# Dilated attention with the tokens stored by residue: fewer score blocks, and the two heads of a pair on the two halves of the array

## The reference

```python
ATTN_GROUPS = ((128, 1), (512, 4), (2048, 16))
...
    s = jnp.einsum('brhnqd,brhnkd->brhnqk', qb, kk) * (dh ** -0.5) + bias
    s = jnp.where(valid, s, -jnp.inf)
    mx = jnp.max(s, axis=-1, keepdims=True)
    p = jnp.exp(s - mx)
    l = jnp.sum(p, axis=-1)
    o = jnp.einsum('brhnqk,brhnkd->brhnqd', p, vv) / l[..., None]
    lse = mx[..., 0] + jnp.log(l)
...
    wts = jax.nn.softmax(jnp.stack(lses, axis=0), axis=0)
    y_b = jnp.sum(wts[..., None] * jnp.stack(outs, axis=0), axis=0)
```

## Time and profile before

| | |
|---|---|
| median of 3 runs | 2230.58 us |
| the profiled execution, its span | 2225.15 us, 2223.2 us |
| busy share of the span: PE, DVE, ACT, POOL | 96%, 48%, 30%, 13% |
| mean granted TensorE clock | 0.983 of 2.4 GHz |
| attention stage (the four pairs) | 404 to 736 us from the start |

### The profile page before, as it was taken

How to read it: one execution, slowest core, us unless ns; L and a number is a source line. 1 busy time by engine, 2 the same in 40 slices (tenths; PEclk the granted TensorE clock), 3 DMA queues, 4 the chain that set the end, 5 groups by cost and what they waited for, 6 DMA issues and landing times.

```text
span 2223.2 us, 24553 instructions
## 1 busy us (share of the span) xinstructions
PE 2144.5 (96%) x9948; PEld 1713.2 (77%) x9948; DVE 1077.8 (48%) x1707; ACT 656.9 (30%) x1069; POOL 295.0 (13%) x214
## 2 busy tenths in 40 slices
PE   6999999999999999999998899999999999999997
PEld 5777788777777888888877567777777778888886
DVE  6566543444445644343454655235555644434344
ACT  4333322222223432222233222023343334222222
POOL 3122210111111111010020001120010112001012
PEclk9999999999999999999998999899999999999998
DMA  4222233322221333333321222231111132333331
GB/s 146 70 76 76 81 112 98 79 69 69 72 78 38 95 91 99 95 96 104 93 79 60 67 67 67 76 105 47 48 48 39 48 104 69 102 95 95 99 91 67
DMA packets 53312, 178.33 MB, mean 80 GB/s; under 512 B 5975, under 2 KB 7255, under 8 KB 53200
## 3 DMA queue, kind: packets, MB, share of 16 engines
q1 hardware_dynamic: 52480, 175.61, 26.0%
q10 hardware_dynamic: 720, 1.16, 0.1%
HBM read 174.46 MB, written 2.28 MB: 79 GB/s over the span
## 4 chain that ended last, share of the span: by engine, by line
PE 90%; DVE 6%; ACT 2%; issue 1%; POOL 0%; DMA 0%; SPq 0%; DVEq 0%; POOLq 0%
PE PS L881 25%; PE PS L883 24%; PE PS L882 24%; PE PS L1016 2%; PE PS L1039 2%; PE PS L1143 2%; PE PS L1170 2%; PE PS L1025 1%; PE PS L1118 1%; PE PS L994 1%; PE PS L981 1%; DVE WL L1454 1%; PE PS L1096 1%; PE PS L946 1%; PE PS L1078 1%
## 5 line engine op out<-in xcount | busy, mean ns | idle before, releaser
L881 PE MATMUL PS<-HH,WH 128*128 128x512 f32 x1368 | 561.1, 410 | 14.6 <-DVE WL L1454 11.9
L883 PE MATMUL PS<-HH,WL 128*128 128x512 f32 x1368 | 538.2, 393 | 0.0
L882 PE MATMUL PS<-HL,WH 128*128 128x512 f32 x1368 | 536.8, 392 | 0.0
L881 PE MATMUL PS<-AH,WH 128*128 128x512 f32 x1096 | 445.1, 406 | 10.4 <-DVE WL L1454 8.5
L1454 DVE TENSOR_TENSOR WL<-RAW,WH 128x1024 fp32r<-128x1024 f32 (+2 forms) x257 | 324.9, 1264 | 256.9 <-ACT WH L1214 256.4
L1214 ACT ACTIVATE WH<-RAW 128x1024 fp32r<-128x1024 f32 (+2 forms) x320 | 325.4, 1017 | 365.0 <-PE PS L883 316.6
L883 PE MATMUL PS<-AH,WL 128*128 128x512 f32 x1096 | 431.9, 394 | 0.0
L882 PE MATMUL PS<-AL,WH 128*128 128x512 f32 x1096 | 431.5, 394 | 0.0
L881 PEld LDWEIGHTS PS<-HH,WH 128*128 128x128 f32 x1368 | 259.2, 189 | 79.5 <-issue 14.4
L883 PEld LDWEIGHTS PS<-HH,WL 128*128 128x128 f32 x1368 | 258.9, 189 | 56.4
L882 PEld LDWEIGHTS PS<-HL,WH 128*128 128x128 f32 x1368 | 259.9, 190 | 50.0 <-issue 1.0
(11 more groups left out here) (224 smaller groups left out, 1794.9 us busy)
## 6 DMA issues: line engine op xcount, KB each, us to landing
RAW<-wst SPq DMA_DIRECT2D x296, 512.0 KB, 3.5
RAW<-wst SPq DMA_DIRECT2D x16, 384.0 KB, 3.0
AR<-scr SPq DMA_DIRECT2D x16, 256.0 KB, 4.5
RAW<-wst SPq DMA_DIRECT2D x16, 256.0 KB, 2.5
XT<-xT SPq DMA_DIRECT2D x3, 512.0 KB, 8.1
AR<-scr SPq DMA_DIRECT2D x8, 128.0 KB, 5.3
out<-XT SPq DMA_DIRECT2D x4, 256.0 KB, 2.0
out<-XT ACTq DMA_DIRECT2D x4, 256.0 KB, 2.1
```

The lines of the kernel that those rows point to most:

```text
L881: T.matmul(out, wh, XH[:, k, :], start=k == 0, stop=False)
L882: T.matmul(out, wh, XL[:, k, :], start=False, stop=False)
L883: m = T.matmul(out, wl, XH[:, k, :], start=False, stop=k == nk - 1)
```

## The change

Groups 1 and 2 have dilations 4 and 16, so a query meets only keys of its own residue modulo 4. Their q, k and v are now stored by residue: DVE writes the evicted sums of these units through a view that puts the four residues one after the other (`by_residue`), and a block of 128 then holds one residue. A query block needs two blocks of group 0 (one for the first), one of group 1 and one of group 2: 15 blocks a head. An item is now a pair and a block b, with both heads.

Each matmul of a step is issued for head 0 and then head 1. For the scores the heads lie on the two halves of the partitions and write two banks; for the products with the values the value block (64 columns) is stationary, the turned probabilities (128 columns) move, and the heads write the two halves of the partitions of one bank. The result stands turned already, so `turn_yb` goes.

A query block of group 0 holds other tokens than one of groups 1 and 2, so there are two softmaxes, with their own maxima and sums, and `merge` joins them in three steps once a pair: `choose_strips` (DVE) and `unfold` (one matmul, then eight dependent DVE instructions with one exponential on ACT) bring the second softmax's statistics into token order and give each its share; `shares` spreads them with 16 matmuls of a column by the identity, and `split_yb` multiplies, adds and splits. For a pair this stands within the first block of the next one, for the last pair at its end.

`Fill` has 10 places for nine units (18 for the eight of the last pair), not 26 weighted ones, and before the scores of the next pair's first block the units are drained. A bias vector has 384 values and is made in one piece. The table of constants grows by 136 columns.

```diff
-        for p in range(2):
-            e.turn_bank("vector", g, p)
-            e.bias_vector(g, p)
+        e.turn_bank("vector", g)
+        e.bias_vector(g)
...
+def merge(e, hp, step):
+
+    if step == 0:
+        e.choose_strips(hp)
+    elif step == 1:
+        e.hold(4, "unfolded", hp)
+        e.unfold(hp)
+    elif step == 2:
+        for x in (0, 1):
+            e.turn_bank("share", hp, x)
+        e.shares(hp)
+        e.split_yb(hp)
+
+
+def ask(e, hp, b):
+    for i in (0, 1):
+        e.hold(SB[i], "qk", hp, b, i)
+    e.attention_scores(hp, b)
...
 def attention_pair(e, hp, units):
-    items = [(hp, i, n) for i in (0, 1) for n in ORD_N]
-    fill = Fill(e, units, 26)
-
-    def ask(it):
-        for g in range(3):
-            e.hold(SB[g], "qk", it, g)
-        e.attention_scores(it)
-
-    ask(items[0])
-    e.attention_softmax(items[0])
-    for m, it in enumerate(items):
-        w = WORK[it[2]]
-        then = items[m + 1] if m < 7 else None
-        fill(w)
-        if then:
-            ask(then)
-        fill(w)
-        blocks = 2 * (it[2] + 1) + min(2, it[2] + 1)
-        for b in range(0, blocks, 4):
-            if b == 8:
-                fill(w)
-            e.turn_bank("turn", it, b)
-            e.attention_turn(it, b, min(4, blocks - b))
-        if then:
-            e.attention_softmax(then)
-        fill(w)
-        e.hold(OB, "pv", it)
-        e.attention_out(it, blocks)
+    fill = Fill(e, units, 10 if hp < 3 else 18)
+    for b in range(4):
+        if hp and b == 0:
+            merge(e, hp - 1, 0)
+        fill()
+        if b < 3:
+            ask(e, hp, b + 1)
+        elif hp < 3:
+            fill.drain()
+            ask(e, hp + 1, 0)
+        if hp and b == 0:
+            merge(e, hp - 1, 1)
+        fill()
+        for i in (0, 1):
+            e.turn_bank("turn", hp, b, i)
+            e.attention_turn(hp, b, i)
+        if b < 3:
+            e.attention_softmax(hp, b + 1)
+        elif hp < 3:
+            e.attention_softmax(hp + 1, 0)
+        if hp and b == 0:
+            merge(e, hp - 1, 2)
+        fill()
+        e.hold(OB, "pv", hp, b)
+        e.attention_out(hp, b)
+        if hp == 3 and b == 3:
+            for step in range(3):
+                merge(e, 3, step)
+                fill(2)
     fill.drain(hp == 3)
-    e.turn_bank("yb", hp)
-    e.turn_yb(hp)
...
+    ask(e, 0, 0)
+    e.attention_softmax(0, 0)
...
+            def bias_vector(s, g):
+                b = s.bank["vector", g]
+                s.free("vector", g)
...
+                t = T.matmul(PS[0:24, b, 0:384], tab[0:33, :], oh[0:33, g * 384:(g + 1) * 384], start=True, stop=True)
...
-            def attention_scores(s, it):
-                hp, i, n = it
-                sl, W, k0, p = SLOT[hp % 2], 128 * (n + 1), max(0, n - 1), slice(64 * i, 64 * i + 64)
+            def attention_scores(s, hp, b):
+                sl = SLOT[hp % 2]
                 for g in range(3):
                     pe.wait_ge(*at("free", "sum", unit_of("ka", 4 * g + hp)))
-                for x, (g, ka, w) in enumerate(((1, 0, W), (2, 0, W), (0, k0 * 128, W - k0 * 128))):
+                s.free("qk", hp, b, 0)
+                s.free("qk", hp, b, 1)
+                for g, k, n, a in ((0, max(0, b - 1), min(2, b + 1), score_column(b)), (1, b, 1, 256), (2, b, 1, 384)):
                     o = 3 * g * 512
-                    s.free("qk", it, x)
-                    t = T.matmul(PS[:, SB[x], 0:w], sl[p, o + n * 128:o + n * 128 + 128],
-                                 sl[p, o + 512 + ka:o + 512 + ka + w], start=True, stop=True)
-                    t.then_inc(*pe_done["attn"].next("scored", it, x))
-
-            def attention_turn(s, it, m, c):
-                b, Sx = s.bank["turn", it, m], SS[ORD_N.index(it[2]) % 2]
-                s.free("turn", it, m)
-                pe.wait_ge(*at("p", it))
-                for q in range(c):
-                    t = T.transpose(PS[:, b, q * 128:(q + 1) * 128], Sx[:, (m + q) * 128:(m + q + 1) * 128], ident())
...
-            def attention_out(s, it, blocks):
-                hp, i, n = it
-                s.free("pv", it)
...
+                t.then_inc(*pe_done["attn"].next("p_turned", hp, b, i))
+
+            def attention_out(s, hp, b):
+                s.free("pv", hp, b)
                 for g in range(3):
                     pe.wait_ge(*at("free", "tokens", unit_of("va", 4 * g + hp)))
-                keys = [(1, j) for j in range(n + 1)] + [(2, j) for j in range(n + 1)] + \
-                       [(0, j) for j in range(max(0, n - 1), n + 1)]
-                for m, (g, j) in enumerate(keys):
-                    if m % 4 == 0:
-                        pe.wait_ge(*at("free", "turn", it, m))
-                    o = (3 * g + 2) * 512 + j * 128 + 64 * i
-                    t = T.matmul(PS[:, OB, 0:64], PT[:, m * 128:(m + 1) * 128], SLOT[hp % 2][:, o:o + 64], start=m == 0,
...
+                pe.wait_ge(*at("free", "turn", hp, b, 0))
+                pe.wait_ge(*at("free", "turn", hp, b, 1))
+                blocks = [(0, 0, b - 1, b > 0, False), (0, 128, b, b == 0, True), (1, 256, b, True, False),
+                          (2, 384, b, False, True)]
+                for g, c, j, first, last in blocks[b == 0:]:
+                    o, x = (3 * g + 2) * 512 + j * 128, min(g, 1) * 128
+                    for i in (0, 1):
+                        t = T.matmul(PS[64 * i:64 * i + 64, OB, x:x + 128], SLOT[hp % 2][:, o + 64 * i:o + 64 * i + 64],
+                                     PT[:, 512 * i + c:512 * i + c + 128], start=first, stop=last)
+                t.then_inc(*pe_done["attn"].next("pv", hp, b))
...
+            def unfold(s, hp):
+                s.free("unfolded", hp)
+                pe.wait_ge(*at("strips", hp))
+                t = T.matmul(PS[:, 4, 0:64], con("unfold"), strips, start=True, stop=True)
...
+            def shares(s, hp):
+                pe.wait_ge(*at("share", hp))
+                for x in (0, 1):
+                    b = s.bank["share", hp, x]
+                    s.free("share", hp, x)
+                    for n in range(4):
+                        for i in (0, 1):
+                            c = 8 * x + 2 * n + i
+                            t = T.matmul(PS[64 * i:64 * i + 64, b, n * 128:(n + 1) * 128],
+                                         spread_column(share[:, c:c + 1], 64), ident(), start=True, stop=True)
...
+            def attention_softmax(s, hp, b):
+                act.wait_ge(*at("max", hp, b))
+                for i in (0, 1):
+                    for x, a in ((0, score_column(b)), (2, 256)):
+                        P = SS[b % 2][:, 512 * i + a:512 * i + (512 if x else 256)]
+                        t = A.activation(P, P, ACT.Exp, bias=ST[hp % 2][:, x, 0, b, i:i + 1],
+                                         accum_out=ST[hp % 2][:, x, 1, b, i:i + 1])
+                t.then_inc(*act_done["attn"].next("p", hp, b))
+
+            def attention_turn(s, hp, b, i):
+                if i:
...
+                    t = A.activation(PT[:, 512 + a:1024], PS[:, s.bank["turn", hp, b, i], a:512], ACT.Copy, scale=1.0)
...
+            def attention_out(s, hp, b):
+                act.wait_ge(*at("pv", hp, b))
+                t = A.activation(OT[:, :, b * 128:(b + 1) * 128],
+                                 PS[:, OB, 0:256].rearrange("p (x c) -> p x c", x=2), ACT.Copy, scale=1.0)
...
-                    s.scaled(i, dst, scale=0.125 if name == "qa" else None).then_inc(*bank_read.next(*free))
+                    scale, view = 0.125 if name == "qa" else None, by_time if j > 3 else None
+                    s.scaled(i, by_residue(dst) if view else dst, 0, 128, scale, view).then_inc(*bank_read.next(*free))
...
+            def attention_turn(s, hp, b, i):
+                if i == 0:
...
+                    t = V.tensor_copy(PT[:, a:512], PS[:, s.bank["turn", hp, b, i], a:512])
...
+            def choose_strips(s, hp):
+                raw, mask = stats[:, 48 * (hp % 2) + 32:48 * (hp % 2) + 48], con("strip")
+                dve.wait_ge(*at("p", hp, 3))
+                t = V.tensor_tensor(strips.rearrange("p (n c) -> p n c", n=4),
+                                    bass.AP(raw.tensor, raw.offset, [list(raw.ap[0]), [0, 4], [1, 16]]),
+                                    bass.AP(mask.tensor, mask.offset, [list(mask.ap[0]), [1, 4], [0, 16]]), ALU.mult)
+                t.then_inc(*dve_done["attn"].next("strips", hp))
...
+                dve.wait_ge(*at("unfolded", hp))
+                V.tensor_tensor(own.rearrange("p (m i r) -> p m i r", m=8, i=2),
+                                PS[:, 4, 0:64].rearrange("p (m r i) -> p m i r", m=8, i=2), mask, ALU.mult).then_inc(
+                    *dve_done["attn"].next("free", "unfolded", hp))
...
+                V.tensor_reduce(st[:, 1].rearrange("p k b i -> p b k i"),
...
+                V.tensor_tensor(low.rearrange("p (b i) -> p b i", b=4), st[:, 0, 0], st[:, 1, 0], ALU.min).then_inc(
```

(4 more changed lines are left out.)

241 lines of the change are left out of this document (129 added, 112 removed).

## The result

The changed kernel takes 2153.38 us, median of four runs (2151.37 to 2155.53), against 2229.36 us before (2227.74 to 2230.81, one run more than the three shown at the start): a ratio of 0.966, 95% interval 0.9643 to 0.9676, or 76 us less. Predicted were 2157.5 us, 2148 to 2181. The two profiled executions take 2225.15 and 2151.37 us, 73.8 us apart; the sum of the prediction was 73.1.

A forecast was written before the change was run, and what follows sets the result against it. PE was taken to bound the attention stage. 74.0 us less PE work, minus 6.0 of waits, plus 5.1 from bias vectors, took 73.1 off 2225.15, to 2152.0 us; 5.4 more for the median gave 2157.5, range 2148 to 2181.

The forecast's parts named there:

- Scores, turning, products, merge: PE's rewritten work in the attention stage: 74.0 us less in sum if the two heads' matmuls run side by side.
- Rival 2: Products and shares: column halves pay for their weight loads, 9 to 18 us, about 14, time 2171.5 us; chance 0.06.
- Stalls: New PE waits in the attention stage, at pair ends, shares and pb: 6.0 us back, between 0 and 12.
- pair ends: End of three pairs: products wait for a copy out of PSUM, 0.93 us each, 2.8 us together.
- the shares: Block 0 of three pairs: shares wait for DVE's copy from their bank, 0.7 us each, 2.1 together.
- The wait before pb's last block: After the last pair, split_yb with DVE's evictions in between: 1 us allowed.
- rival 3: Attention blocks and merges: dependent chains on DVE and ACT exposed oftener, 13 us more, 2170.5 us; chance 0.14.
- about 264: Attention stage from the first scores to pb: should last about 264 us, covered by PE except for the named waits.
- Strided evictions: DVE's strided writes of groups 1 and 2: nothing on the path, evictions staying near 0.7 us.
- Bias vectors: First stage: no wait for the first vector's second piece, clock regained, shorter pieces; 5.1 us gained, between 0 and 7.
- The clock's 1.7 us: Ten us after the first bias vector: the clock's fall goes with PE's idle time, regaining 1.7 us.
- The median: Whole kernel: 5.4 us added because the median of runs lay that far above the profiled execution, giving 2157.5 us.

The follow-up runs named there:

- e1: Changed kernel with scores, products and shares all issued head after head instead of alternating: 2166.26 us, attention stage 277.57 us against 261.41.
- e3: Changed kernel with only the products with the values issued head after head: 2159.04 us, attention stage 268.00 us against 261.41.
- e2: Changed kernel with only the scores issued head after head: 2162.25 us, attention stage 268.85 us against 261.41.
- e6: Changed kernel with the evictions of groups 1 and 2 written in order, without the stride: 2151.77 us, attention stage 261.44 us against 261.41.
- e4: Changed kernel with each bias vector made in two pieces again, each with a bank in turn: 2158.6 us, ratio to before 0.9689.
- e5: Kernel before the change with the two pieces of each bias vector in banks of their own: 2220.27 us, ratio to before 0.9969.
- e11: Changed kernel with a block's three steps in one visit, v units last, first half of the shares in bank 4: 2146.17 us, attention stage 253.55 us.

## Why the prediction was right

**Scores, turning, products, merge: 74.0 us.** Measured 134.2 - 60.9 = 73.3 (60.9 is the sum of the table's four rows "after", scores to merge). The price by distances between starts, a straight line in the columns plus one amount a group, held for all four kinds to 0.5 us. What carried it is that the halves run side by side; single pairs in the second layer had said so, and e1 to e3 put 16.2 us on it, at the order as written. A strict separation was not tried; as an estimate from e2's overlap, it would have cost about 0.33 us more at each border.

**Rival 2, weight loads of the column halves.** Within e3's products the passes of one head follow each other every 0.109 us on the same column half, while each weight load takes 0.137 us and begins within 0.002 us of the start of the pass before it; in the order as changed, two such streams alternate, and eight products take 1.02 us as predicted. The loads are hidden. The Trainium skill (TensorE: Matmul & The Clock Gate, Part 3) says in its list of what overlaps that a load runs beside a matmul only when their row groups differ, while its text on the mechanism also lets a load go ahead into a background weight buffer. These passes use the same rows and overlap: the measurement differs from the list, and decides.

**Stalls: 6.0 us predicted, 4.3 measured.** The place was right for the pair ends and the shares. The pair ends were 0.15 us too dear each, 0.09 of it because ACT's copy of 512 columns takes 0.596 us and I had taken the 0.686 of DVE's. The wait before pb's last block was an allowance and did not come. That a merge's chain could hold DVE so long that a turning waits 1.2 us for a token bank was missed; this is rival 3, once in 20 places. The stage, 262.7 by the sum and "about 264" in the text, was 1.3 us too long by the sum: 1.7 from these waits, less the 0.7 by which the rewritten work gained too little, and 0.3 that no row here accounts for.

**Strided evictions.** The bound was right (e6: nothing), but "near 0.7 us" was wrong: 0.953.

**Bias vectors: 5.1 us.** The wait of 2.81 us was as said (e4 brings back 3.08). The clock's 1.7 us had the mechanism wrong: the fall did not go with the idle time, it moved. From 50 to 80 us the granted clock was 0.83, 0.83 and 0.87, and is 0.77, 1.00 and 0.83, although PE is now covered in all of these 30 us (and was busy for 4.29 of the ten us before them, in both kernels). That is 4.7 us of clock missing before and 4.0 after: 0.7 came back. The whole term still came out: the attention's first scores start 5.4 us earlier, the mLSTM's 5.7. With the spread of some 3 us among variants this cannot be told from 5.1, nor from the 4.1 and 3.75 us of e4 and e5, so the agreement of the sum is in part luck.

**The median.** I added 5.4 us for the distance between the profiled execution of before and its median; of the changed kernel the two lie 2.0 us apart. With the sum within 0.7 us of the profiled difference, this is most of the 4.1 us by which 2157.5 was too high.

## What to carry to other kernels

Where one engine is covered all through a stage, price a rewrite by the distances between that engine's starts, per group and per column, and add up the waits that the new order leaves: here it came out within 1 us of 74. Put work on the two halves of the array in alternating order, and look first for places where a step stands directly behind the one that it needs, and for a bank that two unrelated things share. Steps that stand together save part of their borders: one visit a block, with the next block's scores and the turning between, was worth another 7 us here, 4 of them from borders and 3 from waits.

## What the runs showed of the hardware that I had not expected

- A matmul for the other half of the array starts before earlier passes of the first half are through: in e2 three passes ahead of its place.
- What two groups save by standing together depends on their kinds: products and scores about 0.20 us, scores and turning 0.05 (e11); scores right behind four transposes of a unit (1.72 us in the changed kernel, 0.45 + 1.28 apart) next to nothing.
- DVE: a write of 128 x 512 float32 with a step of 128 elements took 0.953 us, in order 0.689; a multiplication with two reads by residue 1.084 instead of 0.680.
- Two DVE instructions with two operands in SBUF stood still while POOL ran a weight split: 0.175 us became 2.261, and 0.174 became 1.310.
